# First gate chunk of a decoder trunk loaded and split in five pieces instead of four

## The chip, the core and the metric

The kernel runs on one core of a Trainium2 chip. The metric is the device time of one execution in microseconds (us). The core has a matrix engine (PE, with its weight loads listed apart as PEld), a vector engine (DVE), a scalar engine (ACT), a general engine (POOL) and a sequencer that issues most transfers (SP); each runs its own stream of instructions, and they wait for one another by semaphores.

## The reference, cut to what matters

Two layers of a decoder trunk over 256 tokens with a model width of 1024. Each layer adds a feed-forward block, a mixer, a cross attention and a second feed-forward block to the residual stream, each on an RMS-normed input. Only the very first block matters here.

```
D_MODEL, SEQ, D_FF = 1024, 256, 2816
def rmsnorm(x, w):
    y = x * rsqrt(mean(x * x, -1) + 1e-6)
    return y * w
def swiglu(h, w_gate, w_up, w_down):
    return (silu(h @ w_gate) * (h @ w_up)) @ w_down
for layer in range(2):
    x = x + 0.5 * swiglu(rmsnorm(x, norm_w[layer, 0]), ...)   # ffn_w_gate, ffn_w_up, ffn_w_down [layer, 0]
    x = x + mixer(...); x = x + cross_attention(...); x = x + 0.5 * swiglu(...)
return rmsnorm(x, final_norm_w)
```

## The kernel before

**Precision.** Each fp32 operand is split into a high part, which the matrix engine takes as it is, and a low part, the rest. A product is three matrix products: high by high, high by low, low by high. ACT makes the high parts (`w_hi`, the first half of `hT`), DVE subtracts them from the source for the low parts (`w_lo`, the second half of `hT`).

**Chunks.** All weights pass as chunks of 1 MB (2048 fp32 values in each of 128 partitions) through a ring of three slots (`raw`, `w_hi`, `w_lo`). A gate or up chunk is 256 columns of the weight by all 1024 rows, that is eight k-tiles of 128 rows. For such a chunk PE runs, for each k-tile, two products of `w_hi` with both parts of `hT` (512 columns, line 1975, `wide_hi`) and two of `w_lo` with the high part (256 columns, line 1982, `wide_lo`). A feed-forward block has eleven rounds of a gate, an up and a down chunk.

**The start.** Nothing can be computed until the first gate chunk and the input, transposed and k-tile by k-tile, are there. The host lays both side by side in one array `first`: eight columns with the norm's weights, then four quarters, each with two k-tiles of the input (512 columns) and the same two k-tiles of the gate weight (512 columns). SP issues the four quarters (line 615), then the first up chunk in two halves (line 619), the second gate chunk (line 629), a block of constants (line 633) and the input in rows (line 635). Later chunks are issued when DVE has split the chunk that held their ring slot (`lo_done`).

For each quarter (`start` on ACT and on DVE, and the first lines of `ffn` on PE):
- ACT waits until the quarter has landed, makes the high part of the input for each of its two k-tiles, scaled by the norm's weights (line 739), and then the high part of the weight, 512 columns at once (line 741);
- DVE makes the two low parts of the input (line 1267), then the low part of the weight, 512 columns at once (line 1296);
- PE waits for both low parts of the input (`turned_done`) and the high weight, runs four products of 512 columns, waits for the low weight, and runs four of 256.

After the four quarters ACT and DVE split the up chunk in two halves (lines 727 and 1281), and PE goes on with it. Ahead of the first quarter PE runs ten products of a constant (line 2658).

**The first down chunk.** The first chunk that needs the result of the gate and up products is the first down chunk. ACT copies the row of norms from PSUM (line 751), splits the first half of that down chunk (line 727), does the gate's activation (line 802), and DVE at last makes the low part of the hidden values (line 1375), which the first down product on PE (line 1954) waits for.

The order on each engine is that in which the code is written; there is no scheduler.

Of the kernel before, what the change touches and what calls it, by code (L numbers as in the profile page):

```python
# [20 lines left out]
F32 = mybir.dt.float32  # L21
# [6 lines left out]
P = 128  # L28
SEQ, MEM, D = 256, 256, 1024
TT = SEQ // P  # L30
KT = D // P
# [87 lines left out]


FFN_CHUNKS = 3 * FJ
EVEN_ORDER = ["x0", "x1", "x2", "q0", "q1", "k0", "k1", "v0", "v1", "g0", "g1", "z0", "z1"]
ODD_ORDER = ["s", "w", "c", "qn0", "qn1", "qs0"]

# [38 lines left out]
def build(nc, d, out):  # L163
# [3 lines left out]
    with ctx:  # L167
# [15 lines left out]
        def sem(name):  # L183
            return ctx.enter_context(nc.semaphore(name))
# [107 lines left out]
        turned_hi_done, turned_done = sem("turned_hi_done"), sem("turned_done")  # L292
        mem_row_mm, mem_row_done = sem("mem_row_mm"), sem("mem_row_done")
        cols_hi_done, half_done = sem("cols_hi_done"), sem("half_done")
        quarter_in, up_half_in = [sem(f"quarter_in{q}") for q in range(3)], sem("up_half_in")
        quarters_hi, quarters_lo, halves_hi = sem("quarters_hi"), sem("quarters_lo"), sem("halves_hi")
        row_mm, row_read = sem("row_mm"), sem("row_read")
        up_copied, up_read = sem("up_copied"), sem("up_read")
        silu_done = sem("silu_done")
# [127 lines left out]

        def first_part(i, ks):

            at_ = KT + (ks.start // 2) * 4 * SEQ + 2 * i * SEQ + (ks.start % 2) * SEQ  # L430
            return first_in[:, at_:at_ + (ks.stop - ks.start) * SEQ]

        gu_hi, gu_lo, gu_hi_last, gu_lo_last = (
            arena_r[:, i * 512:(i + 1) * 512].rearrange("p (k c) -> p k c", k=2) for i in range(4))
# [158 lines left out]
        def _(sp):  # L593
# [13 lines left out]
            def ffn(layer, which, first=False):  # L607
                base = at["ffn", layer, which]
                gate, up = (d[w][layer, which].rearrange("(k p) (j c) -> j p k c", p=P, c=CW)
                            for w in ("ffn_w_gate", "ffn_w_up"))  # L610
                down = d["ffn_w_down"][layer, which].rearrange("(j k p) c -> j p k c", k=2, p=P)
                if first:
                    for q in range(4):
                        qs = slice(q and KT + 4 * q * SEQ, KT + 4 * (q + 1) * SEQ)
                        sp.dma_start(first_in[:, qs], d["first"][:, qs])\
                          .then_inc(raw_in[0] if q == 3 else quarter_in[q], 16)
                    for kh in range(2):
                        ks = slice(4 * kh, 4 * kh + 4)
                        sp.dma_start(slot_k(base + 1, CW)[:, ks, :], d["first_up"][:, ks, :])\
                          .then_inc(raw_in[1] if kh else up_half_in, 16)  # L620
                else:
                    load(base, slot_k(base, CW), gate[0])
                    load(base + 1, slot_k(base + 1, CW), up[0])
                def turn(j):
                    for c, (w, width, row) in enumerate(((gate, CW, j + 1), (up, CW, j + 1), (down, D, j))):
                        n = base + 2 + c
                        if not (first and isinstance(j, int) and j == 0 and c == 0):
                            sp.wait_ge(lo_done, j * 3 + (n - RING + 1))
                        sp.dma_start(slot_k(n, width),
                                     w[bass.ds(row, 1)].rearrange("a p k c -> (a p) k c"))\  # L630
                          .then_inc(raw_in[n % RING], 16)
                        if first and isinstance(j, int) and j + c == 0:
                            sp.dma_start(consts[:, 0:P], d["consts"][:, 0:P]).then_inc(ident_in, 16)
                            for t in range(TT):
                                sp.dma_start(x[:, t, :], d["x"][0, t * P:(t + 1) * P, :]).then_inc(x_in[t], 16)

                if first:

                    turn(0)
                    turn(1)  # L640
                    sp.dma_start(mem_rows, d["mem"][0].rearrange("(t p) c -> p t c", p=P)).then_inc(mem_in, 16)
                    sp.dma_start(norm_cols[:, :], d["norm_cols"]).then_inc(norm_cols_in, 16)
                    sp.dma_start(turned_raw, d["memT"][:, :, :]).then_inc(memT_in, 16)
                    tables = small_loads()
                    for j in range(2, 6):
                        turn(j)
                        for dst, src in tables[3 * (j - 2):3 * (j - 1)]:
                            sp.dma_start(dst, src).then_inc(small_in, 16)
                    for j, (a, b) in ((6, (0, 4)), (7, (4, 7))):
                        turn(j)  # L650
                        with nc.allow_non_contiguous_dma(reason="a few KB of per-channel columns"):
                            for dst, src in strided_loads()[a:b]:
                                sp.dma_start(dst, src).then_inc(small_in, 16)
                with sp.Fori(8 if first else 0, FJ - 1) as j:
# [21 lines left out]
        def _(act):  # L676
# [52 lines left out]
                made[0] = n + kh  # L729

            def start():
                for q in range(4):
                    cs = slice(q * CHUNK // 4, (q + 1) * CHUNK // 4)
                    if q < 3:
                        act.wait_ge(quarter_in[q], 16)
                    else:
                        act.wait_ge(raw_in[0], landed(0))
                    for k in range(2 * q, 2 * q + 2):
                        nc.scalar.activation(hT_hi[:, k, :], first_part(0, slice(k, k + 1)), ACT.Copy,
                                             scale=first_in[:, k:k + 1]).then_inc(turned_hi_done, 1)  # L740
                    nc.scalar.activation(w_hi[:, 0, cs], first_part(1, slice(2 * q, 2 * q + 2)), ACT.Copy)\
                      .then_inc(quarters_hi if q < 3 else hi_done, 1)
                act.wait_ge(up_half_in, 16)
                hi_half(1, 0)
                act.wait_ge(raw_in[1], landed(1))
                hi_half(1, 1)
# [465 lines left out]
        def _(dve):  # L1212
# [51 lines left out]
            def turned_lo(at_, hi, lo, src, weight):  # L1264

                dve.wait_ge(turned_hi_done, at_ + 1)
                V.scalar_tensor_tensor(lo, src, weight, hi.bitcast(F32), ALU.mult, ALU.subtract).then_inc(turned_done, 1)  # L1267
# [17 lines left out]
                made[0] = n + kh  # L1285

            def start():
                for q in range(4):
                    cs = slice(q * CHUNK // 4, (q + 1) * CHUNK // 4)
                    for k in range(2 * q, 2 * q + 2):  # L1290
                        turned_lo(k, hT_hi[:, k, :], hT_lo[:, k, :], first_part(0, slice(k, k + 1)), first_in[:, k:k + 1])
                    if q < 3:
                        dve.wait_ge(quarters_hi, q + 1)
                    else:
                        dve.wait_ge(hi_done, 1)
                    V.tensor_tensor(w_lo[:, 0, cs], first_part(1, slice(2 * q, 2 * q + 2)), w_hi[:, 0, cs].bitcast(F32),
                                    ALU.subtract)\
                     .then_inc(quarters_lo if q < 3 else lo_done, 1)
                lo_half(1, 0)
                lo_half(1, 1)  # L1300

# [647 lines left out]
        def _(pe):  # L1949
# [165 lines left out]
            def ffn(layer, which):  # L2115
# [7 lines left out]
                v = norm_no(layer, 3 * which)  # L2123
                w = SETS.get(("norm", layer, 3 * which))
                if f == 0:
                    for q in range(4):
                        ks = range(2 * q, 2 * q + 2)
                        pe.wait_ge(turned_done, 2 * q + 2)
                        if q < 3:
                            pe.wait_ge(quarters_hi, q + 1)  # L2130
                        else:
                            pe.wait_ge(hi_done, 1)
                        wide_hi(0, 0, ks=ks)
                        if q < 3:
                            pe.wait_ge(quarters_lo, q + 1)
                        else:
                            pe.wait_ge(lo_done, 1)
                        last = wide_lo(0, 0, ks=ks)
                    used(last)
                    pe.wait_ge(halves_hi, 1)  # L2140
                    wide_hi(1, 2, ks=range(4))
                    pe.wait_ge(hi_done, 2)
                    wide_hi(1, 2, ks=range(4, KT))
                    pe.wait_ge(lo_done, 2)
                    used(wide_lo(1, 2))
                elif ("norm", layer, 3 * which) in FILL:
                    pe.wait_ge(hT_done, 4 * w + 4)
# [563 lines left out]
```

## Time and profile before

| | |
|---|---|
| Time, median of 3 runs | 1218.43 us (1217.64 to 1219.44) |
| The profiled execution | 1217.78 us |
| Span in its profile, first to last instruction | 1215.9 us |
| Matrix engine (PE) busy | 1204.8 us, 99% of the span |
| Vector engine (DVE) busy | 797.8 us, 66% |
| Scalar engine (ACT) busy | 644.5 us, 53% |
| DMA, mean over the span | 177 GB/s |

The span is that of the instructions; the profiled execution's own time is 1.88 us longer. A busy PE here means that a product is under way at any time, not that it runs at its peak; where the products follow one another without a gap, a shorter path to the first of them is what can move the whole.

### The profile page before, as it was taken

The page shows a single profiled execution, that of the slowest core. Times are in us where ns is not written, and L with a number is a line of the kernel's source. Part 1 is how long each engine was busy: PE and PEld are TensorE (multiplying, and loading weights), DVE is VectorE, ACT ScalarE, POOL GpSimd, SP SyncE. Part 2 cuts the span into 40 slices and gives each one's busy share as a digit, 9 for nine tenths or more (in the row PEclk, how much of TensorE's full clock was granted, in tenths as well). Part 3 has the DMA queues.
Part 4 walks back from the last instruction along what each step waited for, and adds up shares of the span by engine and source line. Part 5 has one row for each costly group of instructions (what it writes and reads, how often), then busy time and mean ns, then how long its engine had stood idle before and what let it go on. Part 6 is the DMA issues. An engine that isn't in the chain of part 4 may idle for free.

```text
span 1215.9 us, 18049 instructions
## 1 busy us (share of the span) xinstructions
PE 1204.8 (99%) x7179; PEld 1057.8 (87%) x7179; DVE 797.8 (66%) x859; ACT 644.5 (53%) x873; POOL 111.6 (9%) x112
## 2 busy tenths in 40 slices
PE   9999999999999999999999999999999999999997
PEld 8888889989889888888898888899978898888886
DVE  6766766864668566666676666666785685666664
ACT  7554556553456554444464444454676565544443
POOL 1010001640113110000020000020000131100001
PEclk9999999999999999999999999999999999999999
DMA  9966664554444375656556565644632343756560
GB/s 317 344 192 203 176 205 140 161 186 139 140 146 165 105 234 181 196 183 200 177 177 206 176 201 178 202 143 146 201 120 83 128 156 110 251 178 200 178 205 35
DMA packets 166929, 214.76 MB, mean 177 GB/s; under 512 B 14816, under 2 KB 144992, under 8 KB 166752
## 3 DMA queue, kind: packets, MB, share of 16 engines
q1 hardware_dynamic: 166592, 213.29, 54.3%
q8 instruction: 34, 0.56, 0.2%
q0 software_dynamic: 144, 0.52, 0.1%
q10 hardware_dynamic: 144, 0.26, 0.1%
q14 instruction: 15, 0.12, 0.0%
HBM read 213.02 MB, written 1.05 MB: 176 GB/s over the span
## 4 chain that ended last, share of the span: by engine, by line
PE 96%; DVE 2%; ACT 1%; issue 0%; DMA 0%; POOL 0%; POOLq 0%; DVEq 0%; ACTq 0%
PE ps L1975 28%; PE ps L1954 15%; PE ps L1955 15%; PE ps L1956 15%; PE ps L1982 15%; PE ps L2039 1%; PE ps L2623 1%; PE ps L2495 1%; DVE w_lo L1227 1%; PE ps L2645 1%; PE ps L2587 0%; PE ps L2584 0%; DMA arena<-in_first 0%; PE ps L2102 0%; PE ps L2350 0%
## 5 line engine op out<-in xcount | busy, mean ns | idle before, releaser
L1975 PE MATMUL ps<-hT,w_hi 128*128 128x512 f32 x1568 | 374.8, 391 | 1.5 <-DVE hT L1267 1.3
L1975 PEld LDWEIGHTS ps<-hT,w_hi 128*128 128x128 f32 x1568 | 290.0, 188 | 59.5 <-DVE hT L1267 1.5
L1382 DVE TENSOR_TENSOR w_lo<-raw,w_hi 128x2048 fp32r<-128x2048 f32 x108 | 247.6, 2293 | 61.8 <-ACT w_hi L822 61.8
L1227 DVE TENSOR_TENSOR w_lo<-raw,w_hi 128x2048 fp32r<-128x2048 f32 x85 | 195.6, 2308 | 72.7 <-ACT w_hi L692 72.7
L692 ACT ACTIVATE w_hi<-raw 128x2048 fp32r<-128x2048 f32 x85 | 162.3, 1915 | 97.1 <-PE ps L1956 95.6
L1982 PEld LDWEIGHTS ps<-hT,w_lo 128*128 128x128 f32 x1568 | 201.6, 191 | 8.0
L822 ACT ACTIVATE w_hi<-raw 128x2048 fp32r<-128x2048 f32 x108 | 206.1, 1908 | 0.4 <-DMA raw<-in_ffn_w_gate 0.4
L1982 PE MATMUL ps<-hT,w_lo 128*128 128x256 f32 x1568 | 204.0, 283 | 0.0
L1954 PE MATMUL ps<-w_hi,arena_r 128*128 128x512 f32 x354 | 138.3, 391 | 0.0
L1955 PE MATMUL ps<-w_lo,arena_r 128*128 128x512 f32 x354 | 137.8, 389 | 0.0
L1956 PE MATMUL ps<-w_hi,arena_r 128*128 128x512 f32 x354 | 137.4, 388 | 0.0
L1954 PE MATMUL ps<-w_hi,hT 128*128 128x512 f32 (+2 forms) x304 | 105.4, 347 | 0.0
L1955 PE MATMUL ps<-w_lo,hT 128*128 128x512 f32 (+2 forms) x304 | 104.5, 344 | 0.0
L1956 PE MATMUL ps<-w_hi,hT 128*128 128x512 f32 (+2 forms) x304 | 104.4, 344 | 0.0
L1852 POOL TENSOR_SCALAR msq<-msum 128x1 f32<-128x1 f32 x18 | 27.8, 1547 | 811.9 <-ACT xn L702 729.4
L795 ACT ACTIVATE arena<-ps 128x512 f32<-128x512 f32 x44 | 26.4, 600 | 121.8 <-PE ps L1982 121.8
L814 ACT ACTIVATE arena_r<-arena 128x512 fp32r<-128x512 f32 x44 | 27.9, 633 | 112.3 <-PE ps L1956 105.7
L809 ACT ACTIVATE arena<-ps 128x512 f32<-128x512 f32 x44 | 26.3, 598 | 107.1 <-PE ps L1982 107.1
L1956 PEld LDWEIGHTS ps<-w_hi,arena_r 128*128 128x128 f32 x354 | 66.5, 188 | 14.0
L1954 PEld LDWEIGHTS ps<-w_hi,arena_r 128*128 128x128 f32 x354 | 66.6, 188 | 12.5
L1955 PEld LDWEIGHTS ps<-w_lo,arena_r 128*128 128x128 f32 x354 | 66.7, 188 | 12.0
L1363 DVE TENSOR_TENSOR arena<-arena,ps 128x512 f32<-128x512 f32 x44 | 30.3, 688 | 57.7 <-ACT arena L809 57.7
(312 smaller groups left out, 1656.8 us busy)
## 6 DMA issues: line engine op xcount, KB each, us to landing
raw<-in_ffn_w_down SPq DMA_DIRECT2D x44, 1024.0 KB, 4.9
raw<-in_ffn_w_gate SPq DMA_DIRECT2D x43, 1024.0 KB, 5.4
raw<-in_ffn_w_up SPq DMA_DIRECT2D x43, 1024.0 KB, 5.3
raw<-in_xattn_wkv SPq DMA_DIRECT2D x16, 1024.0 KB, 5.3
raw<-in_even_w_in SPq DMA_DIRECT2D x13, 1024.0 KB, 5.3
raw<-in_xattn_wq SPq DMA_DIRECT2D x8, 1024.0 KB, 5.0
raw<-in_xattn_wo SPq DMA_DIRECT2D x8, 1024.0 KB, 5.1
raw<-in_odd_w_in SPq DMA_DIRECT2D x8, 1024.0 KB, 5.5
```

Source lines behind the costliest of these rows:

```text
L692: ins = nc.scalar.activation(hi, src, ACT.Copy)
L814: nc.scalar.activation(dst, gu.rearrange("p (k c) -> p k c", k=2), ACT.Copy).then_inc(gu_hi_done, 1)
L822: nc.scalar.activation(w_hi[:, m % RING, :], raw[:, m % RING, :], ACT.Copy).then_inc(hi_done, 1)
L1227: ins = V.tensor_tensor(lo, src, hi.bitcast(F32), ALU.subtract)
L1363: V.tensor_tensor(up, up_lo, ps[:, 2:4, 0:SEQ], ALU.add).then_inc(up_read, 1)
L1382: V.tensor_tensor(w_lo[:, m % RING, :], raw[:, m % RING, :], w_hi[:, m % RING, :].bitcast(F32), ALU.subtract).then_inc(lo_done, 1)
L1852: step(G.tensor_scalar(msq[:, t:t + 1], msum[:, sum_at(v, t):sum_at(v, t) + 1], msum[:, sum_at(v, t) + 1:sum_at(v, t) + 2], EPS, ALU.add, ...
L1954: mm(dst, l_hi, r_hi, start=start, stop=False)
L1955: mm(dst, l_hi, r_lo, start=False, stop=False)
L1956: return mm(dst, l_lo, r_hi, start=False, stop=stop)
L1975: mm(ps[:, bank0 + m, :], cols(w_hi, n, k, CW, m * P, (m + 1) * P), hT[:, k, :, :].rearrange("p a c -> p (a c)"), start=k == 0, stop=False)
L1982: last = mm(ps[:, bank0 + m, SEQ:], cols(w_lo, n, k, CW, m * P, (m + 1) * P), hT[:, k, 0, :], start=False, stop=k == KT - 1)
```

## The change

The first gate chunk and the input beside it come in five pieces instead of four quarters: the first two hold one k-tile of the input and of the weight each, the other three hold two, as before. The host lays the array `first` accordingly, SP issues five transfers, and ACT, DVE and PE go through the five pieces with waits of their own. In the diff the first `start` is ACT's, the second DVE's, and the last part is PE's.

```
+PIECES = [range(0, 1), range(1, 2), range(2, 4), range(4, 6), range(6, 8)]
...
         def first_part(i, ks):
 
-            at_ = KT + (ks.start // 2) * 4 * SEQ + 2 * i * SEQ + (ks.start % 2) * SEQ
-            return first_in[:, at_:at_ + (ks.stop - ks.start) * SEQ]
+            piece = next(p for p in PIECES if ks.start in p)
+            at_ = KT + (2 * piece.start + i * len(piece) + ks.start - piece.start) * SEQ
+            return first_in[:, at_:at_ + len(ks) * SEQ]
...
-                    for q in range(4):
-                        qs = slice(q and KT + 4 * q * SEQ, KT + 4 * (q + 1) * SEQ)
+                    for q, ks in enumerate(PIECES):
+                        qs = slice(q and KT + 2 * ks.start * SEQ, KT + 2 * ks.stop * SEQ)
                         sp.dma_start(first_in[:, qs], d["first"][:, qs])\
-                          .then_inc(raw_in[0] if q == 3 else quarter_in[q], 16)
+                          .then_inc(raw_in[0] if q == 4 else piece_in[q], 16)
...
             def start():
-                for q in range(4):
-                    cs = slice(q * CHUNK // 4, (q + 1) * CHUNK // 4)
-                    if q < 3:
-                        act.wait_ge(quarter_in[q], 16)
+                for q, ks in enumerate(PIECES):
+                    cs = slice(ks.start * CW, ks.stop * CW)
+                    if q < 4:
+                        act.wait_ge(piece_in[q], 16)
                     else:
                         act.wait_ge(raw_in[0], landed(0))
-                    for k in range(2 * q, 2 * q + 2):
-                        nc.scalar.activation(hT_hi[:, k, :], first_part(0, slice(k, k + 1)), ACT.Copy,
+                    for k in ks:
+                        nc.scalar.activation(hT_hi[:, k, :], first_part(0, range(k, k + 1)), ACT.Copy,
                                              scale=first_in[:, k:k + 1]).then_inc(turned_hi_done, 1)
-                    nc.scalar.activation(w_hi[:, 0, cs], first_part(1, slice(2 * q, 2 * q + 2)), ACT.Copy)\
-                      .then_inc(quarters_hi if q < 3 else hi_done, 1)
+                    nc.scalar.activation(w_hi[:, 0, cs], first_part(1, ks), ACT.Copy)\
+                      .then_inc(pieces_hi if q < 4 else hi_done, 1)
...
             def start():
-                for q in range(4):
-                    cs = slice(q * CHUNK // 4, (q + 1) * CHUNK // 4)
-                    for k in range(2 * q, 2 * q + 2):
...
+                for q, ks in enumerate(PIECES):
+                    cs = slice(ks.start * CW, ks.stop * CW)
+                    for k in ks:
...
-                    V.tensor_tensor(w_lo[:, 0, cs], first_part(1, slice(2 * q, 2 * q + 2)), w_hi[:, 0, cs].bitcast(F32),
+                    V.tensor_tensor(w_lo[:, 0, cs], first_part(1, ks), w_hi[:, 0, cs].bitcast(F32),
                                     ALU.subtract)\
-                     .then_inc(quarters_lo if q < 3 else lo_done, 1)
+                     .then_inc(pieces_lo if q < 4 else lo_done, 1)
...
                 if f == 0:
-                    for q in range(4):
-                        ks = range(2 * q, 2 * q + 2)
-                        pe.wait_ge(turned_done, 2 * q + 2)
...
+                    for q, ks in enumerate(PIECES):
+                        pe.wait_ge(turned_done, ks.stop)
...
```

On ACT, the start of the program before, from the first wait for a transfer (`arena` is the buffer that holds the landed pieces; `hT` rows are the input, `w_hi` rows the weight):

```order
L739 ACTIVATE hT<-arena 128x256 [waits quarter_in0]
L739 ACTIVATE hT<-arena 128x256
L741 ACTIVATE w_hi<-arena 128x512
L739 ACTIVATE hT<-arena 128x256 [waits quarter_in1]
L739 ACTIVATE hT<-arena 128x256
L741 ACTIVATE w_hi<-arena 128x512
```

The same stretch of ACT in the changed kernel, where the lines stand two further down:

```order
L741 ACTIVATE hT<-arena 128x256 [waits piece_in0]
L743 ACTIVATE w_hi<-arena 128x256
L741 ACTIVATE hT<-arena 128x256 [waits piece_in1]
L743 ACTIVATE w_hi<-arena 128x256
L741 ACTIVATE hT<-arena 128x256 [waits piece_in2]
L741 ACTIVATE hT<-arena 128x256
L743 ACTIVATE w_hi<-arena 128x512
```

The first group of three has become two groups of two, with a wait and a weight split of 256 columns each; what stands behind them is as before.

On PE, the same place before, behind the ten products of a constant:

```order
L1975 MATMUL ps<-hT,w_hi 128x512 [waits quarters_hi,turned_done]
L1975 MATMUL ps<-hT,w_hi 128x512 x3
L1982 MATMUL ps<-hT,w_lo 128x256 [waits quarters_lo]
L1982 MATMUL ps<-hT,w_lo 128x256 x3
L1975 MATMUL ps<-hT,w_hi 128x512 [waits quarters_hi,turned_done]
```

And in the changed kernel:

```order
L1977 MATMUL ps<-hT,w_hi 128x512 [waits pieces_hi,turned_done]
L1977 MATMUL ps<-hT,w_hi 128x512
L1984 MATMUL ps<-hT,w_lo 128x256 [waits pieces_lo]
L1984 MATMUL ps<-hT,w_lo 128x256
L1977 MATMUL ps<-hT,w_hi 128x512 [waits pieces_hi,turned_done]
```

The eight products of the first quarter are in two groups of four, each behind two waits; their number is the same. On SP one transfer has become two at the head of the queue, and everything else stands one place later:

```order
L617 DMA arena<-in_first 128x520
L617 DMA arena<-in_first 128x512
L617 DMA arena<-in_first 128x1024 x3
L621 DMA raw<-in_first_up 128x1024 x2
L631 DMA raw<-in_ffn_w_gate 128x8x256
```

Ahead of these two rows of half size stood one of 128x1032 and three of 128x1024.

## Rows read from the trace of the kernel before

**Rows 1.** The page's chain that ended last, by engine.
```profile
PE 96%; DVE 2%; ACT 1%; issue 0%; DMA 0%; POOL 0%; POOLq 0%; DVEq 0%; ACTq 0%
```

**Rows 2.** Waits of PE, 30 us to the end: us in total, times, longest.
```profile
PE ps L2250 <- DVE arena L1454: 1.6, 2, 0.8
PE ps L1954 <- DVE q_parts L1467: 0.7, 2, 0.4
```

**Rows 3.** PEld's timeline at the start: start us, us, what, count, idle before.
```profile
6.48 0.76 PEld L1975 LDWEIGHTS ps<-hT,w_hi 128*128 128x128 f32 x4 [1.49 <-DVE hT L1267]
...
10.72 0.76 PEld L1975 LDWEIGHTS ps<-hT,w_hi 128*128 128x128 f32 x4
```

**Rows 4.** SP's timeline: issue of the first, second and fourth quarter, and the constants.
```profile
0.74 0.39 SPq L615 DMA_DIRECT2D arena<-in_first  x1
...
1.19 0.42 SPq L615 DMA_DIRECT2D arena<-in_first  x1
...
2.13 0.43 SPq L615 DMA_DIRECT2D arena<-in_first  x1
...
4.38 3.08 SPq L633 DMA_DIRECT2D consts<-in_consts  x1
```

**Rows 5.** Issues with us to landing: first, second and fourth quarter, in that order.
```profile
arena<-in_first SPq DMA_DIRECT2D x1, 516.0 KB, 4.2
...
arena<-in_first SPq DMA_DIRECT2D x1, 512.0 KB, 5.0
...
arena<-in_first SPq DMA_DIRECT2D x1, 512.0 KB, 6.7
```

**Rows 6.** ACT's timeline: quarters one (input), two (input and weight) and four (input).
```profile
4.93 0.91 ACT L739 ACTIVATE hT<-arena 128x256 fp32r<-128x256 f32 x2 [2.69 <-DMA arena<-in_first]
...
6.27 0.89 ACT L739 ACTIVATE hT<-arena 128x256 fp32r<-128x256 f32 x2
7.07 0.62 ACT L741 ACTIVATE w_hi<-arena 128x512 fp32r<-128x512 f32 x1
...
8.92 0.90 ACT L739 ACTIVATE hT<-arena 128x256 fp32r<-128x256 f32 x2
```

**Rows 7.** DVE's timeline: quarter two (input, weight) and quarter four (input).
```profile
7.00 0.88 DVE L1267 SCALAR_TENSOR_TENSOR hT<-arena,hT 128x256 fp32r<-128x256 f32 x2
7.80 0.69 DVE L1296 TENSOR_TENSOR w_lo<-arena,w_hi 128x512 fp32r<-128x512 f32 x1
...
9.79 0.88 DVE L1267 SCALAR_TENSOR_TENSOR hT<-arena,hT 128x256 fp32r<-128x256 f32 x2
```

**Rows 8.** Groups by line, 0 to 30 us: count, busy us, mean ns, idle before.
```profile
L739 ACT ACTIVATE hT<-arena 128x256 fp32r<-128x256 f32 x8 | 3.6, 496 | 2.7 <-DMA arena<-in_first 2.7
L1267 DVE SCALAR_TENSOR_TENSOR hT<-arena,hT 128x256 fp32r<-128x256 f32 x8 | 3.5, 481 | 5.5 <-ACT hT L739 5.5
L1296 DVE TENSOR_TENSOR w_lo<-arena,w_hi 128x512 fp32r<-128x512 f32 x4 | 2.8, 688 | 0.0
L741 ACT ACTIVATE w_hi<-arena 128x512 fp32r<-128x512 f32 x4 | 2.5, 616 | 0.0
```

**Rows 9.** DMA in 5 to 8 us, then in 11.5 to 14.2 us: packets by size, rate.
```profile
DMA packets 318, 1.16 MB, mean 386 GB/s; under 512 B 35, under 2 KB 35, under 8 KB 318
...
DMA packets 936, 0.99 MB, mean 368 GB/s; under 512 B 32, under 2 KB 893, under 8 KB 936
```

**Rows 10.** The first down chunk: SP's issue, its landing, ACT's, DVE's and PE's rows.
```profile
13.78 0.38 SPq L629 DMA_DIRECT2D raw<-in_ffn_w_down  x1
...
raw<-in_ffn_w_down SPq DMA_DIRECT2D x1, 1024.0 KB, 10.6
...
24.38 1.06 ACT L727 ACTIVATE w_hi<-raw 128x1024 fp32r<-128x1024 f32 x1
...
28.35 0.68 DVE L1375 TENSOR_TENSOR arena_r<-arena,arena_r 128x512 fp32r<-128x512 f32 x1
...
29.27 0.19 PEld L1954 LDWEIGHTS ps<-w_hi,arena_r 128*128 128x128 f32 x1
```

More of the change, by code:

```diff
@@ L294, in build @@
         cols_hi_done, half_done = sem("cols_hi_done"), sem("half_done")
-        quarter_in, up_half_in = [sem(f"quarter_in{q}") for q in range(3)], sem("up_half_in")
-        quarters_hi, quarters_lo, halves_hi = sem("quarters_hi"), sem("quarters_lo"), sem("halves_hi")
+        piece_in, up_half_in = [sem(f"piece_in{q}") for q in range(4)], sem("up_half_in")
+        pieces_hi, pieces_lo, halves_hi = sem("pieces_hi"), sem("pieces_lo"), sem("halves_hi")
         row_mm, row_read = sem("row_mm"), sem("row_read")
@@ L1287, in start @@
             def start():
-                for q in range(4):
-                    cs = slice(q * CHUNK // 4, (q + 1) * CHUNK // 4)
-                    for k in range(2 * q, 2 * q + 2):
-                        turned_lo(k, hT_hi[:, k, :], hT_lo[:, k, :], first_part(0, slice(k, k + 1)), first_in[:, k:k + 1])
-                    if q < 3:
-                        dve.wait_ge(quarters_hi, q + 1)
+                for q, ks in enumerate(PIECES):
+                    cs = slice(ks.start * CW, ks.stop * CW)
+                    for k in ks:
+                        turned_lo(k, hT_hi[:, k, :], hT_lo[:, k, :], first_part(0, range(k, k + 1)), first_in[:, k:k + 1])
+                    if q < 4:
+                        dve.wait_ge(pieces_hi, q + 1)
                     else:
                         dve.wait_ge(hi_done, 1)
-                    V.tensor_tensor(w_lo[:, 0, cs], first_part(1, slice(2 * q, 2 * q + 2)), w_hi[:, 0, cs].bitcast(F32),
+                    V.tensor_tensor(w_lo[:, 0, cs], first_part(1, ks), w_hi[:, 0, cs].bitcast(F32),
                                     ALU.subtract)\
-                     .then_inc(quarters_lo if q < 3 else lo_done, 1)
+                     .then_inc(pieces_lo if q < 4 else lo_done, 1)
                 lo_half(1, 0)
@@ L2125, in ffn @@
                 if f == 0:
-                    for q in range(4):
-                        ks = range(2 * q, 2 * q + 2)
-                        pe.wait_ge(turned_done, 2 * q + 2)
-                        if q < 3:
-                            pe.wait_ge(quarters_hi, q + 1)
+                    for q, ks in enumerate(PIECES):
+                        pe.wait_ge(turned_done, ks.stop)
+                        if q < 4:
+                            pe.wait_ge(pieces_hi, q + 1)
                         else:
@@ L2133, in ffn @@
                         wide_hi(0, 0, ks=ks)
-                        if q < 3:
-                            pe.wait_ge(quarters_lo, q + 1)
+                        if q < 4:
+                            pe.wait_ge(pieces_lo, q + 1)
                         else:
@@ L2698 @@
             ("first", np.concatenate([np.reshape(inputs["norm_w"][0, 0], (KT, P)).T]
-                                     + [columns_by_k(a)[:, 2 * q:2 * q + 2, :].reshape(P, -1) for q in range(4)
+                                     + [columns_by_k(a)[:, ks.start:ks.stop, :].reshape(P, -1) for ks in PIECES
                                         for a in (np.transpose(inputs["x"][0]), inputs["ffn_w_gate"][0, 0][:, 0:CW])], axis=1)),
```

## Prediction

> **What bounds the kernel now.** I read the page's chain first: PE holds 96% of it [rows 1]. Then the waits of PE: from 30 us to the end it stands for 2.3 us in all, each time for DVE [rows 2]. So from there on the kernel is one row of products, and anything that lets the first one start earlier, without a gap behind it, moves the end by as much. The waits that matter are at the start. PE's first weight load comes at 6.48, after 1.49 us of standing, released by DVE; that of the fourth quarter comes at 10.72 [rows 3]. That is (10.72 - 6.48) / 3 = 1.41 us a quarter.
>
> I then looked for what sets that pace, from the transfers upwards. Quarter one is issued at 0.74 and lands 4.2 us later, at 4.94, which is when ACT starts (4.93); quarter two lands at 1.19 + 5.0 = 6.19, and ACT takes it up at 6.27; quarter four lands at 2.13 + 6.7 = 8.83, and ACT takes it up at 8.92 [rows 4 to 6]. The landings are (8.83 - 6.19) / 2 = 1.32 us apart, and ACT needs (8.92 - 6.27) / 2 = 1.33 us for a quarter. DVE takes up quarter two at 7.00 and quarter four at 9.79: 1.40 us a quarter [rows 7]. So four things run nearly abreast: transfers 1.32, ACT 1.33, DVE 1.40, PE 1.41. Only the first quarter's landing is waited for in full; behind it ACT is 0.08 to 0.09 us late for each landing, and DVE, which starts quarter two 0.24 us after ACT has made its first part (6.27 + 0.49 = 6.76), trails a little more.
>
> **The first half-size piece.** It brings 258 KB rather than 516. Its landing is bounded below by half the time of the quarter (0.74 + 2.1 = 2.84, if all of the 4.2 us went by bytes) and above by 4.93 (nothing won). I take the steady rate of 386 GB/s [rows 9]: 264 kB less are 0.68 us, so 4.25. From a landing to PE there is one input split on ACT (496 ns) and one on DVE (481 ns) [rows 8], about 0.1 us of hand-overs with them, so PE starts near 5.35, some 1.1 us earlier than now, where it waits for two of each.
>
> **What the early start is worth.** It is worth what is left of it when the last piece has been worked off, and the bytes ahead of that one are the same. The third piece (k-tiles 2 and 3) holds what quarter two held, ends at the same byte of the stream, and so lands at 6.19; the fifth lands at 8.83 as quarter four did. Piece two ends where quarter one ended and lands near 4.93. Its half of a quarter's work is 1.41 / 2 = 0.7 us for PE, startable at 4.93 + 0.50 + 0.48 + 0.1 = 6.0. So PE works on k-tiles 0 and 1 between 5.35 and about 6.7 and then stands until piece three has been split. The one wait is cut into several.
>
> What is really won is the small backlog. ACT is done with piece two before 6.19: from 4.93, one input split and one weight split of 256 columns. For that split no row exists; it lies between half of 616 ns and the whole, 0.31 to 0.62 [rows 8]. With the input's 0.50 ACT is free by 6.05 at the latest, so it takes up piece three at about 6.19 instead of 6.27. DVE likewise: its 256-column low weight is between 0.34 and 0.69, and with 0.48 for the input it is free by about 6.6 (4.93 + 0.50 + 0.48 + 0.69), before piece three's first input part at 6.19 + 0.50 = 6.69. So DVE no longer trails there. Its low weight of that piece then waits for ACT: ACT makes the high weight 0.80 us after the piece's start (7.07 - 6.27) and needs 0.62, so it is there at 7.61; the hand-over from ACT to DVE I take as 0.05, which gives 7.66 against 7.80 now [rows 6, 7]. From there DVE is its own bound again, as before, at 1.40 a piece, and everything behind it is 0.14 earlier, PE's load of the last piece too: 10.58 instead of 10.72. ACT could not give more: it takes up the fifth piece at about 8.86, 0.06 earlier, and DVE needs that part only at 9.65.
>
> **What it costs.** No product is added on PE, only one more pair of waits. ACT and DVE each get one instruction more, ahead of piece three, where both have the time as worked out; were piece two to land after about 5.2, that cover would be gone and DVE would pass its lateness on. SP issues one transfer more, about 0.46 us at the present spacing (1.19 - 0.74), so all that is queued behind it (both up halves, the second gate chunk, the constants, the input's rows) is issued that much later. The fourth quarter, issued at 2.13, could not move before the third had gone through, at about 7.5, so 0.46 us is hidden by some 5 us of queue. The constants' issue held SP for 3.08 us [rows 4]; if the longer queue made the second gate chunk's issue stand as long, it would be out by about 7.9, still ahead of the bytes in front of it, two quarters and two up halves of 1.3 us each behind the 6.19, to 11.4. Last, the first two pieces move in runs of half the length. For the price I take the nearest stretches: 386 GB/s with long packets and 368 where 893 of 936 packets were the 1 KB ones of a weight chunk [rows 9]. For 524 kB that is at most 524/368 - 524/386 = 1.42 - 1.36 = 0.07 us, and at least nothing. All later landings shift by it. The sum is 0.14 less 0 to 0.07: 0.07 to 0.14 us won. I take **0.1 us**.
>
> **A ceiling further on.** The first down chunk is issued at 13.78 and lands 10.6 us later, at 24.38, and ACT starts on it at 24.38; the low hidden part that hangs on it is done by DVE at 29.03, and PE loads for the product at 29.27 [rows 10]. That landing is set by the queue of transfers, not by PE. So PE can be at most about 0.2 us earlier there before it waits, whatever was won ahead.
>
> **A rule that speaks against the change.** Each transfer, by the row, took 4.2 us where its bytes at the steady rate are 528/386 = 1.37, so 2.8 us are start and finish. The Trainium skill, in "DMA: Bandwidth & Descriptors", section "Anatomy of one DMA", puts a fixed cost of about 2.0 us on each (for the path through the general engine's queue, not SP's), and its section "Rules for kernel authors" asks for 1 MiB or more in one. By that, if the fixed costs stood one behind the other, piece two would come 2.0 us later, and by an estimate from that page the kernel would lose about 1.9 us. The trace disagrees for transfers in a queue: quarters two to four land 1.32 us apart, not 4 [rows 4, 5].
>
> **The rivals.**
> - *The start-ups add* (slower). Place: the second small transfer at the head of the queue. Price: 2.8 us, the part of the first transfer that is not bytes, on every landing behind it; less the 0.14 won, the profiled execution would go from 1217.8 to 1220.4, and the median from 1218.4 to 1221.1. It decides from 0.14 us of delay on (the gain is gone) and passes 0.2% from about 2.6 us. For it speaks that the queue is cold there, against it the spacing of the later quarters. In full I give it 0.03; a part of it, 0.15 to 1.5 us of delay, 0.15, which gives about 1218.5 to 1219.8.
> - *The early start is kept.* If the landings of pieces three to five came earlier too, because the stream itself starts sooner with smaller transfers, PE would keep up to its 1.1 us, until the ceiling cuts it to 0.2: about 1218.2, or 1217.3 if the ceiling moved along. For it: PE's first load is released by just this landing. Against: the bytes ahead are equal. 0.09; a gain beyond 0.2% in any way 0.02.
> - *Nothing remains.* With the full 0.07 of short packets, and a DVE that trails as before, the gain is 0 to 0.05. This can't be told from my forecast by the time, only by the trace; it is inside the 0.71 that is left.
>
> **How the numbers follow.** The profiled execution took 1217.78 us, 1.88 more than its span; 0.1 less is 1217.7. It lay 0.65 under the median, so for the median I say 1218.43 - 0.1 = **1218.3**. The three runs of before spread from 1217.64 to 1219.44, far more than the effect. From 1218.3 the range goes down by 1.1 (the early start kept in full) to 1217.2 and up by 1.2 (most of the partial delays) to 1219.5. About 0.2%, 2.4 us, is what a measurement of this kernel can tell from no change; neither a gain of 1.1 nor a delay of 1.5 reaches it. Faster by more 0.02, within 0.95, slower by more 0.03.
>
> **What the profile would show.** The first transfer lands near 4.25, the second near 4.95, the third to fifth at 6.2, 7.5 and 8.85, each up to 0.07 later. PE's first load comes near 5.35, and it then stands twice or more, nearly a us of it ahead of k-tiles 2 and 3 (load near 7.6 to 7.7); the last piece's load is at 10.58 to 10.65. The down product's load at 29.27 is 0.05 to 0.15 earlier, and from there the two traces run side by side. I would be wrong if the third piece lands before 6.0 or after 6.4, or if the second lands so late that ACT passes its delay on.

## The result, and the profile after

The changed kernel takes 1220.31 us (median of 19 runs, 1218.66 to 1222.38), the kernel before, timed beside it, 1218.24 us (19 runs, 1217.64 to 1221.81). The ratio, taken over all runs and not of the two medians (which are 2.07 us or 0.17% apart), is 1.0013, with a 95% interval of 1.0007 to 1.0019: a small loss, clear of the noise. The time lies above the range of 1217.2 to 1219.5. The profiled execution of the changed kernel has this page head (PE's busy time was 1204.8 us before, the span 1215.9):

```profile
span 1218.3 us, 18053 instructions
## 1 busy us (share of the span) xinstructions
PE 1207.3 (99%) x7179; PEld 1060.5 (87%) x7179; DVE 798.4 (66%) x860; ACT 644.1 (53%) x874; POOL 108.9 (9%) x112
```

The same 7179 products keep PE busy 2.5 us longer, and the span is 2.4 us longer. Some 1.0 of that is lost at the start, 1.4 in the middle.

**The start.** ACT takes up each piece when it has landed, so its timeline shows the landings; it answers to [rows 6]:

```profile
3.37 0.51 ACT L741 ACTIVATE hT<-arena 128x256 fp32r<-128x256 f32 x1 [1.13 <-DMA arena<-in_first]
...
5.04 0.51 ACT L741 ACTIVATE hT<-arena 128x256 fp32r<-128x256 f32 x1 [0.86 <-DMA arena<-in_first]
...
7.35 0.91 ACT L741 ACTIVATE hT<-arena 128x256 fp32r<-128x256 f32 x2 [1.49 <-DMA arena<-in_first]
...
8.68 0.89 ACT L741 ACTIVATE hT<-arena 128x256 fp32r<-128x256 f32 x2
...
10.00 0.90 ACT L741 ACTIVATE hT<-arena 128x256 fp32r<-128x256 f32 x2
```

ACT takes up the first piece 1.56 us before it took up the first quarter (3.37 against 4.93), the second hardly later than it. But the third piece, which ends at the same byte as the old second quarter, is taken up at 7.35 against 6.27, and ACT stands 1.49 us for it. Everything behind it is as late: 10.00 against 8.92 for the last. The chain of waits, early in the span, names the same transfer:

```profile
1.66 5.66 DMA arena<-in_first
```

It was issued at 1.66 and landed at 1.66 + 5.66 = 7.32; forecast was 6.19. PE's weight loads, which answer to [rows 3], and the first down product's, to [rows 10]:

```profile
5.11 0.55 PEld L1977 LDWEIGHTS ps<-hT,w_hi 128*128 128x128 f32 x2
...
6.39 0.54 PEld L1977 LDWEIGHTS ps<-hT,w_hi 128*128 128x128 f32 x2
...
8.89 0.76 PEld L1977 LDWEIGHTS ps<-hT,w_hi 128*128 128x128 f32 x4 [1.39 <-DVE hT L1269]
...
11.74 0.76 PEld L1977 LDWEIGHTS ps<-hT,w_hi 128*128 128x128 f32 x4
...
30.28 0.19 PEld L1956 LDWEIGHTS ps<-w_hi,arena_r 128*128 128x128 f32 x1
```

PE starts at 5.11 instead of 6.48, works on k-tiles 0 and 1, stands for 1.39 us until 8.89, and loads for the last piece at 11.74 instead of 10.72. The 1.02 us are carried on almost unchanged: 30.28 at the down product against 29.27.

**The middle.** The second loss is far from the edit. By microseconds around 826, the view of windows shows, with PE's busy time and number of products behind the length, and the granted clock in the column PEclk:

```profile
core 0: us, PE busy (x) PEld busy (x) DVE busy (x) ACT busy (x) POOL busy (x), PEclk, DMA share, GB/s
825.00:826.00 1.00, 1.00 (x9) 0.96 (x8) 0.84 (x2) 0.80 (x1) 0.00 (x0) 1.00 1.04 360
826.00:827.00 1.00, 1.00 (x6) 0.97 (x6) 0.97 (x3) 1.00 (x1) 0.00 (x0) 0.65 0.54 191
827.00:828.00 1.00, 1.00 (x7) 1.00 (x6) 1.00 (x3) 0.98 (x2) 0.00 (x0) 0.50 0.00 0
828.00:829.00 1.00, 1.00 (x7) 1.00 (x7) 1.00 (x1) 0.86 (x3) 0.00 (x0) 0.50 0.00 0
829.00:830.00 1.00, 1.00 (x7) 1.00 (x7) 0.69 (x1) 0.00 (x0) 0.00 (x0) 0.64 0.00 0
830.00:831.00 1.00, 1.00 (x11) 1.00 (x10) 0.00 (x0) 0.00 (x0) 0.00 (x0) 1.00 0.14 29
```

The clock falls from 2.4 to 1.2 GHz, and PE, busy all the time, gets through 7 products a microsecond instead of 11. The loss is what is left of the span: 2.4 - 1.0 = 1.4 us. The profile before has full clock here, and 32 products in 3.5 us:

```profile
826.00:829.50 3.50, 3.50 (x32) 3.50 (x31) 2.73 (x3) 1.89 (x4) 0.00 (x0) 1.00 0.00 0
```

A fall is seen only where there is a trace. In the other runs a mean clock of 0.997 or less stands for it: of the fourteen profiles of this case the four with a fall have 0.997, the ten without 0.998 or more. Ten of the 19 timed runs have a mean clock of 0.996 or 0.997 and a span of 1218.3 us or more; the best six have 0.998 or 0.999 and 1216.8 to 1217.1. For the kernel before the best runs are at 1215.8 to 1216.1. So about 1.0 us is lost even in the best runs, and in about half of all runs the fall comes on top.

### The profile page after: what moved, and what is told of

Its sections match the earlier page's. It is cut to its first block, busy times and chain, and to the rows that moved or that the text cites. A ratio compares the mean times of both kernels' runs of the same rounds, so it can differ in the third digit from the quotient of the medians.

```text
span 1218.3 us, 18053 instructions
## 1 busy us (share of the span) xinstructions
PE 1207.3 (99%) x7179; PEld 1060.5 (87%) x7179; DVE 798.4 (66%) x860; ACT 644.1 (53%) x874; POOL 108.9 (9%) x112
## 3 DMA queue, kind: packets, MB, share of 16 engines
HBM read 213.02 MB, written 1.05 MB: 176 GB/s over the span
## 4 chain that ended last, share of the span: by engine, by line
PE 96%; DVE 2%; ACT 1%; DMA 0%; issue 0%; POOL 0%; SPq 0%; POOLq 0%; DVEq 0%; ACTq 0%
PE ps L1977 28%; PE ps L1956 15%; PE ps L1957 15%; PE ps L1958 15%; PE ps L1984 15%; PE ps L2041 1%; PE ps L2624 1%; PE ps L2496 1%; DVE w_lo L1229 1%; PE ps L2646 0%; DMA arena<-in_first 0%; PE ps L2588 0%; PE ps L2585 0%; PE ps L2104 0%; PE ps L2351 0%
```

## The experiments

Two questions: what makes the third piece late, and why the clock falls more often. In the diffs PIECES is how ACT, DVE and PE cut the work, LOADS how SP cuts the transfers; in the changed kernel they are the same. Theory A: the transfers alone, through their number (A1) or their short rows (A2). Theory B: the finer work on the engines. Theory C: PE's early products bring the fall of the clock. "Floor" is the span of the best runs of a kernel, 1215.8 to 1216.1 for the kernel before in all comparisons. Ratios are to the kernel before in the same comparison. Landings and loads are those of one profile each: e1 and e8, whose transfers are those of the kernel before, have the last quarter at 9.03 and 9.21 instead of 8.84, so that less than 0.4 us in a single landing tells little.

**e1: four transfers, work in five.**

```
 PIECES = [range(0, 1), range(1, 2), range(2, 4), range(4, 6), range(6, 8)]
+LOADS = [range(0, 2), range(2, 4), range(4, 6), range(6, 8)]
```

> Four transfers as before, but ACT, DVE and PE work in five pieces. Theory A (the second small transfer at the head delays the stream of transfers): the quarters land as before, the second near 6.2 us, the last gate piece's load on PE comes at 10.7 to 10.8, and the time is that of the kernel before within 0.2 us. Theory B (the split work on ACT and DVE costs the time): the landings are as before, but PE's load of the last piece is near 11.7 and the time about 1 us longer.

**e2: five transfers, work in quarters.**

```
+PIECES = [range(0, 2), range(2, 4), range(4, 6), range(6, 8)]
+LOADS = [range(0, 1), range(1, 2), range(2, 4), range(4, 6), range(6, 8)]
```

> Five transfers, but ACT, DVE and PE work in four quarters as before (the first quarter waits for both small transfers). Theory A: the transfer behind the two small ones lands near 7.3 us instead of 6.2, PE's load of the last quarter comes near 11.7, and the time is about 1 us over the kernel before. Theory B: landings near 5.0, 6.2, 7.5, 8.8, PE's load at 10.7 to 10.8, time as before.

e1 took 1217.94 us against 1218.16, ratio 0.9999 (0.9990 to 1.0008), floor 1215.8. Its loads on PE:

```profile
6.13 0.30 PEld L1980 LDWEIGHTS ps<-hT,w_hi 128*128 128x128 f32 x2 [0.90 <-DVE hT L1272]
...
8.00 0.76 PEld L1980 LDWEIGHTS ps<-hT,w_hi 128*128 128x128 f32 x4 [0.37 <-DVE hT L1272]
...
10.85 0.76 PEld L1980 LDWEIGHTS ps<-hT,w_hi 128*128 128x128 f32 x4
...
29.41 0.19 PEld L1959 LDWEIGHTS ps<-w_hi,arena_r 128*128 128x128 f32 x1
```

e2 took 1219.23, ratio 1.0007 (0.9998 to 1.0016), floor 1216.7:

```profile
6.60 0.76 PEld L1980 LDWEIGHTS ps<-hT,w_hi 128*128 128x128 f32 x4 [1.37 <-DVE hT L1272]
9.03 0.76 PEld L1980 LDWEIGHTS ps<-hT,w_hi 128*128 128x128 f32 x4 [0.98 <-DVE hT L1272]
...
11.88 0.76 PEld L1980 LDWEIGHTS ps<-hT,w_hi 128*128 128x128 f32 x4
...
30.42 0.19 PEld L1959 LDWEIGHTS ps<-w_hi,arena_r 128*128 128x128 f32 x1
```

By the trace and the floor (the ratio's interval takes in 1), the five transfers alone bring the whole delay, with all the work in quarters: the stall ahead of k-tiles 2 and 3, the last load at 11.88 (11.74 in the changed kernel), the down load at 30.42. The finer work alone costs nothing in time; its down load is 0.14 us later, but its first quarter had also landed 0.11 later (5.02 against 4.91). Theory B falls.

**e3: the two small pieces second and third.**

```
+PIECES = [range(0, 2), range(2, 3), range(3, 4), range(4, 6), range(6, 8)]
```

> The same sizes in another order: two k-tiles, one, one, two, two, in transfers and in work. Theory A, if it is the cold head of the stream that minds two small transfers: landings near 4.9, 5.6, 6.2, 7.5, 8.8, and the time of the kernel before within 0.2 us. If small transfers cost wherever they stand: the piece behind them lands 1 us late as in the changed kernel (near 8.5), and the time is 1 us over. Theory B: 1 us over, with landings on time.

1218.20 against 1218.16, ratio 1.0000 (0.9991 to 1.0009), floor 1215.9. The last piece lands at 9.36 in the trace, half as late as in the changed kernel (9.88, before 8.84), and the down load is at 29.63.

**e4: each piece in an array of its own in memory,** so that its rows lie one behind the other.

```
-sp.dma_start(first_in[:, qs], d["first"][:, qs])\
+sp.dma_start(first_in[:, qs], d[f"first{q}"][:, :])\
```

> The changed kernel, but each of the five pieces is an array of its own in HBM, so that its rows lie one behind the other instead of 16416 bytes apart. If the delay comes from reading short runs out of wide rows, the third piece lands near 6.2 us, PE's load of the last piece is near 10.6, and the time is 0.1 us under the kernel before. If it comes from the number or the size of the transfers at the head: third landing near 7.3, about 1 us over.

1219.79, ratio 1.0013 (1.0004 to 1.0022), floor 1216.5. The second piece lands at 4.19 instead of 5.02, but the third at 6.93 and the last at 9.77. For the landings behind the two small pieces the layout is worth 0.1 to 0.4 us of the 1.1 at most, no more than single profiles differ.

**e5: the first quarter in two transfers of 64 rows, each row whole (4 KB); work in quarters.** **e6: the first quarter in one transfer, but in rows cut in two (2 KB).**

```
+for rows in (slice(0, 64), slice(64, P)):
+    sp.dma_start(first_in[rows, qs], d["first"][rows, qs])\
```

```
+dst = dst.rearrange("p (a c) -> p a c", a=2)
+src = d["first_cut"][:, :, 0:516]
```

> Four quarters of work, but the first quarter comes in two transfers of 64 partitions each with the full 4 KB rows: one transfer more, no short rows. Theory A1 (the number of transfers at the head makes the stream late): the second quarter lands near 7.3 us and the time is about 1 us over the kernel before. Theory A2 (the short rows of 2 KB make it late): landings near 4.9, 6.2, 7.5, 8.8 as before, time as before within 0.3 us.

> Four transfers and four quarters of work, but the first quarter is read in two runs of 2064 bytes per partition instead of one of 4128: no transfer more, only short runs. Theory A1: landings as before, time as before. Theory A2: the second quarter lands near 7.3 us, the time is about 1 us over.

e5: 1219.78 against 1218.31, ratio 1.0012 (1.0003 to 1.0022), floor 1217.1; quarter two lands at 7.61, the last at 10.17. e6: 1218.76, ratio 1.0000 (0.9991 to 1.0010), floor 1216.4 to 1216.8; quarter two lands at 7.27, the last at 10.07. The floor of e6 is 0.6 to 0.7 us over, less than the 1 expected. So neither A1 nor A2 holds alone: two transfers of long rows (each over half of the partitions) and one transfer of short rows both make the next one land late, by 1.4 and 1.1 us.

**e7: pieces of one, two, two, two and one k-tile.**

```
+PIECES = [range(0, 1), range(1, 3), range(3, 5), range(5, 7), range(7, 8)]
```

> One k-tile in the first piece and one in the last, two in the three between, in transfers and in work. If one short transfer at the head already makes the stream late: the second piece lands near 6.5 instead of 5.6, and the time is about 1 us over the kernel before. If it takes two of them: landings near 3.4, 5.6, 6.9, 8.2, 8.9, PE's load of the last piece near 11.0 with half the work behind it, and the time up to 0.4 us under the kernel before.

1218.37, ratio 0.9999 (0.9990 to 1.0009), floor 1216.1. The second piece lands at 6.40, near the 6.5 of the first expectation, so one short transfer is enough; but the time is not 1 us over. The last piece lands at 9.97, but it is small, and PE gets k-tiles 1 and 2 already at 7.96. Nothing is won. Why the late landings cost so little here is not shown: the one profile, a run with a fall, has the down load at 30.04, 0.77 us late.

**e8: the kernel before with twelve products of a constant instead of ten ahead of the first quarter.**

```
-WARM = 10
+WARM = 12
```

> The kernel before with twelve products of a constant ahead of the first quarter instead of ten, so that PE is busy until about 5.7 to 6.1 us instead of 5.2. Theory C (what PE does in its first 7 us decides when its clock rises and in which runs it falls again near 825 us): more runs with a mean granted clock of 0.997 and a span 1.5 us over the shortest, as in the changed kernel, where before had 5 of 33. Theory D (the share of these runs is chance or comes from the later end of the start): the share stays near 5 of 33. The shortest spans stay at 1215.8 to 1216.1 by both.

1218.40, ratio 1.0002 (0.9993 to 1.0011), floor 1215.8. Four of 11 runs have a mean clock of 0.997, against 4 of 33 of the kernel before beside it, and the profile has a fall at 825. So the fall comes without any change of the transfers; that it comes more often with more work on PE early is not shown by so few runs.

**e9: the changed kernel, with PE held until both small pieces are there.**

```
-pe.wait_ge(turned_done, ks.stop)
+pe.wait_ge(turned_done, max(ks.stop, 2))
...
-    pe.wait_ge(pieces_hi, q + 1)
+    pe.wait_ge(pieces_hi, max(q + 1, 2))
```

> The changed kernel with one thing altered: PE waits for both small pieces before it starts, so that it takes k-tiles 0 and 1 together, at about 6.4 us, as the kernel before takes its first quarter; transfers, ACT and DVE stay in five pieces. Theory that the late stream alone costs, and that PE's early start is only neutral: the runs look as those of the changed kernel, undisturbed span 1216.9, and in about 12 of 19 of them a mean clock of 0.996 to 0.997 with a span above 1218. Theory that PE's early products are what moves the later fall of the clock: the span stays at 1216.9 (the stream is as late), and runs with a mean clock of 0.997 or less become rare, at most 2 in 10, the median then near 1218.8. A rise of the clock later than 6 us in some runs is expected in the second case, at about 1 us each.

1219.34 against 1217.91, ratio 1.0007 (0.9998 to 1.0016), floor 1216.7 to 1217.0. The transfers are as late as in the changed kernel:

```profile
6.06 0.30 PEld L1980 LDWEIGHTS ps<-hT,w_hi 128*128 128x128 f32 x2 [1.12 <-DVE hT L1272]
...
9.01 0.76 PEld L1980 LDWEIGHTS ps<-hT,w_hi 128*128 128x128 f32 x4 [1.49 <-DVE hT L1272]
...
30.38 0.19 PEld L1959 LDWEIGHTS ps<-w_hi,arena_r 128*128 128x128 f32 x1
```

But one run of 11 has a mean clock of 0.997 or less, where the changed kernel has ten of 19, and the profile has no fall:

```profile
826.00:829.50 3.50, 3.50 (x31) 3.47 (x31) 3.46 (x6) 2.97 (x4) 0.00 (x0) 1.00 0.25 85
```

So the early start of PE, which was to bring the gain, goes with the fall. The times stand accordingly, 1219.34 without it and 1220.31 with it, though they were not timed side by side and the intervals of the two ratios overlap. Side by side, e2 (PE not early) has 0 of 11 such runs and e4 (PE early) 6 of 11, both with late transfers. The median I expected, near 1218.8, was missed: five runs lie at 1217.5 to 1217.7 of span with a clock of 0.999 or 1.0. Such a group is found in the kernel before too, 1.3 to 1.9 us above its floor in 26 of 99 runs. No trace shows one of these runs. A late rise of the clock may be behind it: in the profiles of e6, e11 and e12, above their floors by 0.5 to 0.9, 1.5 and 2.9 us with a mean clock of 0.999 or 1.0, the clock rose only at 9.74, 10.46 and 13.74 us, by the trace's record of it (the mean clock leaves out what stands ahead of the first record).

**e10: the last quarter cut in two, not the first.**

```
+PIECES = [range(0, 2), range(2, 4), range(4, 6), range(6, 7), range(7, 8)]
```

> The kernel before with its last quarter, not its first, cut in two transfers and two parts of work (k-tiles 6 and 7 apart). Theory that short rows or one more transfer cost only where they are the first the queue carries: the first three quarters land as before (4.9, 6.2, 7.5), the last piece by 8.9 to 9.1, span 1215.9, ratio 0.999 to 1.001. Theory that any transfer in short rows costs about 1 us to all behind it: the last piece lands near 9.9, the first down product's load moves from 29.3 to about 30.3, span near 1216.9.

1218.01 against 1217.91, ratio 1.0001 (0.9992 to 1.0010), floor 1215.8 to 1216.1. The first three quarters land at 4.95, 6.21 and 7.49, the last piece at 9.35: 0.5 us late, more than the 9.1 expected, but PE has products in hand, and the down load is at 29.28, to 0.01 us that of before.

**e11: a transfer of 64 KB ahead of the four quarters.**

```
+sp.dma_start(consts[:, 0:P], d["consts"][:, 0:P]).then_inc(ident_in, 16)
 for q in range(4):
```

> The kernel before with one transfer of 64 KB (the block of constants, in rows of 512 bytes) moved from behind the second gate chunk to ahead of the four quarters. By bytes alone the quarters land 0.17 us later each (64 KB at 386 GB/s), with one issue of 0.46 us on top at the most: 5.1 to 5.5 for the first, 9.0 to 9.4 for the last, span 1216.0 to 1216.4. Theory that a first transfer which isn't 128 full rows of 4 KB leaves the stream about 1 us late whatever its bytes: the last quarter near 9.9 and span near 1216.9. Theory that the start is latency which another transfer may take on itself: the first quarter not later than 4.9.

1219.94, ratio 1.0011 (1.0002 to 1.0020), floor 1216.3. The tiny transfer lands at 2.59, the quarters at 5.22, 6.51, 8.27 and 9.53: 0.3 us late at first and 0.7 to 0.8 from the third on, between the two expectations. The median is 2.0 us over, the floor 0.2 to 0.5.

**e12: the first two quarters in one transfer of 1 MB.**

```
+PIECES = [range(0, 2), range(2, 4), range(4, 6), range(6, 8)]
+LOADS = [range(0, 4), range(4, 6), range(6, 8)]
```

> The kernel before with its first two quarters in one transfer of 1 MB (rows of 8 KB), the work still in quarters. PE's first load waits for two quarters' bytes, so it comes near 7.6 instead of 6.5. Theory that fewer transfers and longer rows at the head start the stream sooner: all of the first chunk has landed before 8.8, at 8.3 to 8.6, and since only a backlog of one quarter (1.4 us) stands then, PE's load of the last piece is at 11.3 or so; span 1215.9 to 1216.6. Theory that 128 rows of 4 KB are as good as the queue gets: the last piece at 8.8, span 1216.3 to 1216.9.

1221.64, ratio 1.0023 (1.0014 to 1.0032), floor 1216.9. The first chunk is complete at 8.75 against 8.84: fewer and longer is no better for the stream. And PE stands longer first:

```profile
7.70 1.35 PEld L1980 LDWEIGHTS ps<-hT,w_hi 128*128 128x128 f32 x4 [2.47 <-DVE hT L1272]
10.22 1.40 PEld L1980 LDWEIGHTS ps<-hT,w_hi 128*128 128x128 f32 x4
```

Four loads take 1.35 us where they took 0.76: PE is at the lower clock, into the second quarter too; the record has its first rise at 13.74. Five of 11 runs also have a mean clock of 0.996 or 0.997. In this profile the down load comes at 33.17.

No version beats the kernel before.

## Why the prediction was wrong

**The step that failed** is "the bytes ahead of that one are the same [...] ends at the same byte of the stream, and so lands at 6.19", with the "0 to 0.07 us" for runs of half the length. The bytes are the same; the landing was 7.32, past the 6.4 named as a sign of being wrong. The stream of the kernel before, and then of the changed one, from the start to 4.25 us, in 3.25 to 4.25, and from 4.25 to 8.25:

```profile
DMA packets 151, 0.59 MB, mean 139 GB/s; under 512 B 8, under 2 KB 8, under 8 KB 151
...
DMA packets 87, 0.33 MB, mean 326 GB/s; under 512 B 8, under 2 KB 8, under 8 KB 87
...
DMA packets 431, 1.57 MB, mean 393 GB/s; under 512 B 47, under 2 KB 47, under 8 KB 431
```

```profile
DMA packets 276, 0.54 MB, mean 128 GB/s; under 512 B 23, under 2 KB 23, under 8 KB 276
...
DMA packets 69, 0.15 MB, mean 150 GB/s; under 512 B 7, under 2 KB 7, under 8 KB 69
...
DMA packets 402, 1.44 MB, mean 360 GB/s; under 512 B 43, under 2 KB 43, under 8 KB 402
```

In 3.25 to 4.25, when the second small piece is under way, the stream runs at 150 GB/s, and then at 360 instead of 393. At 6.17, when quarter two had landed, the old stream had moved 0.59 + 1.92 x 0.393 = 1.34 MB, the new one 0.54 + 1.92 x 0.360 = 1.23: 0.11 MB or 0.3 us behind. That is the smaller part of 1.15. The third piece ends at 1.05 MB, so by bytes it had passed. When it did land, at 7.32, 0.54 + 3.07 x 0.360 = 1.65 MB were through: 0.6 MB of later pieces had gone ahead of its last bytes, against 0.29 MB before. These 0.3 MB more are 0.8 us at 360 GB/s, and the two parts together are 1.1. So what I overlooked is that the 16 DMA engines of a transfer can come apart, and a landing is then that of the slowest. That is my reading: the trace does not name the engine of a packet. How evenly they run is seen in the 4-byte packets, 16 of which end a transfer: in 5.1 to 5.9 the first of these two rows, of before, has all 16 of quarter two, the second, of after, only 11:

```profile
DMA packets 93, 0.32 MB, mean 394 GB/s; under 512 B 16, under 2 KB 16, under 8 KB 93
```

```profile
DMA packets 79, 0.28 MB, mean 348 GB/s; under 512 B 11, under 2 KB 11, under 8 KB 79
```

Why the engines come apart stays open inside the DMA. What the runs show: it needs something other than one transfer of whole 4 KB rows at the head (e2, e4, e5, e6, e7, and e11 in part), and behind the first quarter it is about half as much (0.5 us on the last landing in e3 and in e10, one profile each).

**The first half-size piece** landed at 3.34, not at 4.25: less of the 4.2 us is fixed than I took. Its price came with the next pieces. Piece two landed at 5.02, as forecast (4.93 to 4.95).

**PE's early start** came (5.11 for 5.35), but the one wait was not cut into several: PE stood once, for 1.22 us instead of 1.32, now ahead of k-tiles 2 and 3. Between pieces one and two it did not stand, since its first products ran at the lower clock (0.55 us for two loads, 0.30 in e9) and filled the time. The stall ahead of k-tiles 2 and 3 ended at 8.89, not at 7.6 to 7.7, that is 1.2 us later, as the landing.

**The work on ACT and DVE** was sized right, and e1 shows that it costs nothing. The weight split of 256 columns takes 0.40 us on ACT and 0.42 on DVE, inside their bounds of 0.31 to 0.62 and 0.34 to 0.69. The 0.14 us to be won from a smaller backlog came too: the third piece lands 1.15 us later than quarter two did (7.32 against 6.17), and PE's load of the last piece is only 1.02 later (11.74 against 10.72), 0.13 less. So of the sum only the term for the landings failed, with 1.15 us in place of 0 to 0.07. (e1 is no test of this gain: there both small pieces are in one transfer, and ACT is busy with them until 6.57, behind the next landing at 6.30.)

**SP's longer queue** was hidden, as forecast: the constants' issue took 0.82 us instead of 3.08 [rows 4], the stall moved to the input's rows:

```profile
0.74 2.29 SPq L617 DMA_DIRECT2D arena<-in_first  x5
...
5.18 0.82 SPq L635 DMA_DIRECT2D consts<-in_consts  x1
6.04 4.11 SPq L637 DMA_DIRECT2D x<-in_x  x2
```

**The ceiling** at the first down chunk was not put to the test, since no kernel came there earlier than before. In the changed kernel the chunk is issued at 14.89 and lands 10.5 us later, at 25.4, 1.0 us later than before; in e9, with the same transfers issued at the same time (14.90), it lands at 24.51. So it is no fixed mark.

**The rivals.** "The start-ups add" was the right one, in part, and I gave 0.15 to it: a delay of 1.0 to 1.2 us on all landings of the first chunk behind the second transfer, within its bounds of 0.15 to 1.5. Its price on the floor, 1.0 us, would have given 1218.3 + 0.1 + 1.0 = 1219.4. The rest, 0.9 us in the median (the median run has a mean clock of 0.997), is the fall of the clock, which stood in none of my cases: I read a busy PE as one of constant rate, and the spread of the three runs, 1.8 us, as mere noise.

**On the clock what is shown and what isn't.** Shown: the fall exists and costs 1.4 us; holding PE back, with the same transfers, makes it rare (e9: 1 of 11; e2, with late transfers and work in quarters: 0 of 11); with late transfers and PE early it is common (10 of 19, and 6 of 11 in e4); of 99 runs of the kernel before, in three comparisons, 16 have a mean clock of 0.997 or less. An early PE is not needed for it: e12, where PE starts late, has 5 of 11 runs with so low a mean clock.

The traces also tie the products at 5 us to the clock at 826 us, by the moment at which the clock rises. In all four profiles with a fall it begins 819.2 us behind the rise: 7.10 and 826.30 in the changed kernel, 5.81 and 825.00 in e1, 6.38 and 825.58 in e7, 5.90 and 825.09 in e8. In these four PE has just run, or is ending, eight products of 24 columns; the product behind them starts at 826.03, 825.31, 825.91 and 825.14, within 0.4 us of the fall. In the other ten profiles the moment 819.2 us behind the rise is at least 1.1 us ahead of that start or 2.5 us behind it, and the clock stays up: 823.88 against 825.07 in the kernel before, and in e5, which rises at 5.94 like e8 but has everything 1.2 us later, 825.14 against 826.34. So whether a run has the fall goes with how the rise stands to the later products. Not shown: why it is 819.2 us, and what sets the rise in a run (4.58 us in e9 and 7.10 in the changed kernel, one profile each).

## What to carry to other kernels

At the head of a queue, do not count on a piece landing when its byte comes: cutting the first transfer won 1.6 us for its first half and cost 1.1 us for all behind it, as read here because a transfer lands with the slowest of its engines. Where an engine is busy from its first instruction to the end, what counts is the last stall of the start, not the first instruction; ask which landing ends that stall, and cut transfers only behind it (e10 lost nothing). And time such an edit by the spans and clocks of many runs, since a shift of a microsecond can decide whether PE's clock falls.

## What the runs showed of the hardware that was not expected

- 64 KB issued first (e11) landed 1.8 us after the issue, 260 KB after 2.6 us, 516 KB after 4.2 us [rows 5]: at most 1.8 us of a first transfer's time are fixed, not the 2.8 that I had worked out.
- The packets of 2 KB of the second small piece began with durations of up to 1.36 us (at 2.72), where most whole rows of the old second quarter took 0.16 us and none over 0.44; before, slow packets (up to 1.18 us) are found only in the first quarter.
- PE's clock fell to 1.2 GHz at 826 us with PE busy without a gap by the profile (which models the ends of products), behind some 5 us of products of 128 columns and eight of 24, and in all four profiles with a fall 819.2 us behind the clock's rise.
- In the changed kernel's profile PE's first products also ran at the lower clock: two loads took 0.55 us at 5.11, and 0.30 at 6.06 in e9. The record has the rise at 7.10 and at 4.58.
